# Layer norms beside two half-by-half projections: square sums and scaled tiles one product later, first sums one product later, inverse root in PSUM

## The reference

```python
mix = (gates[:, :, 0] * y_sb + gates[:, :, 1] * y_ret) @ w_mix_o[l]
x = layer_norm(DN_ALPHA * x + mix, ln1_g[l], ln1_b[l])
xa = memory_cross_attention(x, mem, w_mem_q[l], w_mem_kv[l], w_mem_o[l])
x = layer_norm(DN_ALPHA * x + xa, ln2_g[l], ln2_b[l])
f = x @ w_ffn_in[l]
ff = (jax.nn.silu(f[..., :FFN_HIDDEN]) * f[..., FFN_HIDDEN:]) @ w_ffn_out[l]
x = layer_norm(DN_ALPHA * x + ff, ln3_g[l], ln3_b[l])
```

## Time and profile before

| | us |
|---|---|
| median of 3 runs | 2077.23 (2077.11 to 2078.31) |
| profiled execution, its own time | 2074.83 |
| span of that execution | 2072.8 |
| mean granted clock of PE | 0.988 |
| PE busy | 1976.8 |
| DVE busy | 1100.5 |
| ACT busy | 729.9 |
| POOL busy | 949.3 |

### The profile page before, as it was taken

The page is one execution under the profiler, slowest core; times in us unless marked ns, Lnnn a source line. Parts: engine busy times, 40 slices in busy tenths (PEclk is TensorE's granted clock), DMA queues, the critical chain, the costliest instruction groups (busy, mean ns, idle before and its releaser), DMA issues. The chain is left out here.

```text
span 2072.8 us, 25775 instructions
## 1 busy us (share of the span) xinstructions
PE 1976.8 (95%) x10024; PEld 1638.4 (79%) x10024; DVE 1100.5 (53%) x1180; ACT 729.9 (35%) x1133; POOL 949.3 (46%) x519
## 2 busy tenths in 40 slices
PE   8999999999999999999989999989999999999986
PEld 6888888888777787888768887777888888888866
DVE  5667577400166565238873337877454455411646
ACT  2323224100055555312452224454433333422444
POOL 4243342433354454444575543565555555543423
PEclk9999999999999999999999999999999999999998
DMA  5022020122100000312322111242222222363452
GB/s 187 31 91 71 30 91 31 51 81 71 61 22 21 21 32 21 122 43 78 96 78 72 61 61 59 74 142 92 76 83 87 86 78 82 138 201 129 136 164 97
DMA packets 56538, 168.22 MB, mean 81 GB/s; under 512 B 5888, under 2 KB 12160, under 8 KB 55424
## 3 DMA queue, kind: packets, MB, share of 16 engines
q1 hardware_dynamic: 49648, 142.86, 20.7%
q10 hardware_dynamic: 6800, 24.12, 3.1%
HBM read 142.84 MB, written 24.12 MB: 81 GB/s over the span
## 5 line engine op out<-in xcount | busy, mean ns | idle before, releaser
L508 POOL TENSOR_TENSOR w_hi<-w_raw,one 128x1024 fp32r<-128x1024 f32 x68 | 133.6, 1965 | 467.1 <-PE unit L650 467.1
L650 PE MATMUL unit<-x_hi,w_hi 128*128 128x512 f32 x768 | 248.0, 394 | 13.2 <-DVE diag L1795 9.9
L660 PE MATMUL unit<-x_lo,w_hi 128*128 128x512 f32 x768 | 245.4, 390 | 0.4 <-POOL x_lo L527 0.4
L668 PE MATMUL unit<-x_hi,w_lo 128*128 128x512 f32 x768 | 190.4, 390 | 0.0
L650 PEld LDWEIGHTS unit<-x_hi,w_hi 128*128 128x128 f32 x768 | 144.3, 189 | 45.8 <-issue 11.6
L511 POOL TENSOR_TENSOR w_lo<-w_raw,w_hi 128x1024 fp32r<-128x1024 f32 x68 | 176.6, 2597 | 5.3
L660 PEld LDWEIGHTS unit<-x_lo,w_hi 128*128 128x128 f32 x768 | 144.1, 188 | 31.0 <-POOL x_lo L527 0.9
L668 PEld LDWEIGHTS unit<-x_hi,w_lo 128*128 128x128 f32 x768 | 144.6, 188 | 30.2
L572 POOL TENSOR_TENSOR w_lo<-w_raw,w_hi 128x1024 fp32r<-128x1024 f32 x46 | 112.8, 2451 | 101.3 <-ACT w_hi L1414 101.1
L590 POOL TENSOR_TENSOR beta<-beta,stick 128x128 f32<-128x128 f32 (+7 forms) x64 | 77.1, 1205 | 150.6 <-DVE stick L1936 150.6
L1936 DVE TENSOR_TENSOR_SCAN stick<-stick 128x128 f32<-128x128 f32 (+7 forms) x64 | 106.2, 1661 | 49.8 <-ACT stick L1344 49.8
(11 more groups left out here) (602 smaller groups left out, 5115.8 us busy)
## 6 DMA issues: line engine op xcount, KB each, us to landing
w_raw<-stream SPq DMA_DIRECT2D x157, 512.0 KB, 3.7
w_next<-stream SPq DMA_DIRECT2D x34, 512.0 KB, 4.4
hidden_store<-hidden SPq DMA_DIRECT2D x22, 512.0 KB, 2.6
h_raw<-hidden_store SPq DMA_DIRECT2D x44, 256.0 KB, 3.9
rope_sb<-rope ACTq DMA_DIRECT2D x8, 1024.0 KB, 4.9
w_next<-stream SPq DMA_DIRECT2D x12, 384.0 KB, 3.4
acc<-xT ACTq DMA_DIRECT2D x8, 512.0 KB, 10.3
ret_branch<-acc ACTq DMA_DIRECT2D x8, 512.0 KB, 2.6
```

The source lines that it names most:

```text
L508: pool.tensor_tensor(w_hi[s][:, 0:width], w_raw[:, s, 0:width], one[:].to_broadcast([P, width]), ALU.mult).then_inc(w_hi_done, 1)
L650: x = pe.matmul(out, w_hi[s][:, wk], hi[:, k, cols], start=k == 0, stop=False, skip_group_check=True)
L660: last = pe.matmul(out, w_hi[s][:, wk], lo[:, k, cols], start=False, stop=k == kts - 1 and x_lag > w_lag, skip_group_check=True)
L668: last = pe.matmul(out, w_lo[s][:, wk], hi[:, k, cols], start=False, stop=k == kts - 1 and x_lag <= w_lag, skip_group_check=True)
```

## The change

Five edits, the same in both norms except the last.

1. The square of block q is added to `total_sq` after the residual of block q+1, so a new function `add_square` is split from `residual`; the low parts of the totals go from after q = 7 to after q = 8, the last square of half 1 to the end.
2. `sums(m, 0)` goes from after product 8 to after product 9, and with it the high parts of the totals, mean square and root on ACT, variance and reciprocal on DVE, each one q later.
3. `TILES_BESIDE` spreads the 8 tiles over q = 10 to 15 with 1, 2, 1, 2, 1, 1 tiles, in place of 1, 2, 2, 2, 1 over 9 to 13. ACT takes a tile's steps two q after its entry in place of one, so that tiles 6 and 7 come after the loop, tile 6 ahead of and tile 7 among the weight pieces that follow; POOL's low parts of tiles 6 and 7 likewise.
4. The reciprocal root is written to `aux` bank 2 + half, in PSUM (where the mean square lay), and the scaling reads it there.
5. In `n1` the memory's high part on ACT goes from q = 15 to q = 12, its low part on DVE from q = 14 to q = 13.

```diff
--- before.py
+++ after.py
@@ -74,7 +74,7 @@
 SUMS = (S1, S2, S3, S4)
 RING = 4
 ADDS = KT - 1
-TILES_BESIDE = {9: (0,), 10: (1, 2), 11: (3, 4), 12: (5, 6), 13: (7,)}
+TILES_BESIDE = {10: (0,), 11: (1, 2), 12: (3,), 13: (4, 5), 14: (6,), 15: (7,)}
 TURN_ORDER = (2, 3, 0, 1)
 
 
@@ -194,7 +194,7 @@
             sb(st, "gap4", [P, 2, HALF])
             total_hi, total_lo, total_sq_hi, total_sq_lo = (
                 sb(st, n, [P, HALF], F32R) for n in ("total_hi", "total_lo", "total_sq_hi", "total_sq_lo"))
-            ln_mean2, ln_rstd = sb(st, "ln_mean2", [P, HALF]), sb(st, "ln_rstd", [P, HALF])
+            ln_mean2, ln_var = sb(st, "ln_mean2", [P, HALF]), sb(st, "ln_var", [P, HALF])
         with ExitStack() as st:
             t_hi, t_lo = {}, {}
             for j in (2, 3):
@@ -593,13 +593,23 @@
                         (single_lo if hd else single_hi)(FILL_SPLITS[g])
             split(CH_GSB + 1, CH_MIX + 2 - CH_GSB - 1, 8 * P)
             beside_residual(CH_MIX, CH_MEM, normed_lo)
-            for c in range(CH_MEM + 1, CH_MEM + 6):
+            normed_lo(KT - 2)
+            single_lo(CH_MEM + 1)
+            single_lo(CH_MEM + 2)
+            normed_lo(KT - 1)
+            for c in range(CH_MEM + 3, CH_MEM + 6):
                 single_lo(c)
             for q in range(KT, 2 * KT):
                 normed_lo(q)
             split(CH_MEM + 6, CH_MO + 2 - CH_MEM - 6, 8 * P)
             beside_residual(CH_MO, CH_FFN - 1, normed_part_lo)
-            for f in range(2 * RING):
+            form_lo(0)
+            form_lo(1)
+            normed_part_lo(KT - 2)
+            form_lo(2)
+            form_lo(3)
+            normed_part_lo(KT - 1)
+            for f in range(RING, 2 * RING):
                 form_lo(f)
             for q in range(KT, 2 * KT):
                 normed_part_lo(q)
@@ -939,7 +949,7 @@
                 for q in range(2, 2 * KT):
                     pe.wait_ge(unit_drained[q % 2], first // 2 + max(0, q // 2 - 1))
                     tiles(q, range(KT)).then_inc(unit_ready, 1)
-                    if q == KT:
+                    if q == KT + 1:
                         sums(m, 0)
 
             residual(n1, CH_MIX, U_MIX)
@@ -1436,7 +1446,7 @@
 
             def root(m, hf):
                 act.wait_ge(m.var, hf + 1)
-                act.activation(ln_mean2[:], ln_rstd[:], ACT.Sqrt).then_inc(m.std, 1)
+                act.activation(ln_mean2[:], ln_var[:], ACT.Sqrt).then_inc(m.std, 1)
 
             def beside_residual(m, which, chunk, last_chunk, tile, others):
                 for q in range(1, 2 * KT):
@@ -1448,12 +1458,12 @@
                     if q == KT - 1:
                         act.activation(root_table[:, which:which + 1], one[:], ACT.Sqrt)
                     square_of(m, q - 1)
-                    if q == KT:
+                    if q == KT + 1:
                         total_hi_parts(m, 0)
-                    if q == KT + 1:
+                    if q == KT + 2:
                         mean_square(m, 0)
                         root(m, 0)
-                    for k in TILES_BESIDE.get(q - 1, ()):
+                    for k in TILES_BESIDE.get(q - 2, ()):
                         tile(k)
                     if q in others:
                         others[q]()
@@ -1478,7 +1488,7 @@
                 for k in range(0, KT, 4):
                     act.activation(mem_hi[:, k:k + 4, :], mem_raw[:, k:k + 4, :], ACT.Copy).then_inc(mem_hi_done, 4)
 
-            beside_residual(n1, 0, CH_MIX, CH_MEM, normed_tile, {KT: load_memory, 2 * KT - 1: split_memory})
+            beside_residual(n1, 0, CH_MIX, CH_MEM, normed_tile, {KT: load_memory, KT + 4: split_memory})
 
             def mem_unit(s):
                 return unit[:, s, :].rearrange("p (a t) -> p a t", a=2)[:, :, 0:MEM]
@@ -1543,10 +1553,12 @@
                 if more:
                     queries_and_v(h, base + 4)
 
+            normed_tile(KT - 2)
             single_hi(CH_MEM + 1)
             square_of(n1, 2 * KT - 1)
             total_hi_parts(n1, 1)
             single_hi(CH_MEM + 2)
+            normed_tile(KT - 1)
             keys(0, U_MEM + 1)
             mean_square(n1, 1)
             single_hi(CH_MEM + 3)
@@ -1595,10 +1607,12 @@
                 form_hi_part(1)
 
             beside_residual(n2, 1, CH_MO, CH_FFN - 1, normed_part, {2 * KT - 1: first_forms})
+            normed_part(KT - 2)
             form_hi_part(2)
             form_hi_part(3)
             square_of(n2, 2 * KT - 1)
             total_hi_parts(n2, 1)
+            normed_part(KT - 1)
             for f in range(RING, 2 * RING):
                 form_hi_part(f)
             mean_square(n2, 1)
@@ -2020,6 +2034,9 @@
                     dve.wait_ge(m.total_added, ADDS * hf + n - 1)
                 dve.tensor_tensor(total, acc[:, 0, half(hf)] if n == 1 else total, r, ALU.add
                                   ).then_inc(m.total_added, 1)
+
+            def add_square(m, q):
+                hf, n = divmod(q, KT)
                 dve.wait_ge(m.squared, q + 1)
                 if n > 1:
                     dve.wait_ge(m.square_added, ADDS * hf + n - 1)
@@ -2035,12 +2052,12 @@
 
             def variance(m, hf):
                 dve.wait_ge(m.mean_sq, hf + 1)
-                dve.scalar_tensor_tensor(out=ln_rstd[:], in0=aux[:, 2 + hf, :], scalar=EPS, in1=ln_mean2[:],
+                dve.scalar_tensor_tensor(out=ln_var[:], in0=aux[:, 2 + hf, :], scalar=EPS, in1=ln_mean2[:],
                                          op0=ALU.add, op1=ALU.subtract).then_inc(m.var, 1)
 
             def invert(m, hf):
                 dve.wait_ge(m.std, hf + 1)
-                dve.reciprocal(ln_rstd[:], ln_mean2[:]).then_inc(m.inverted, 1)
+                dve.reciprocal(aux[:, 2 + hf, :], ln_mean2[:]).then_inc(m.inverted, 1)
 
             def center(m, q, freed):
                 hf, k = divmod(q, KT)
@@ -2052,7 +2069,7 @@
             def scale(m, q):
                 dve.wait_ge(m.inverted, q // KT + 1)
                 dve.wait_ge(m.centered, q + 1)
-                dve.tensor_tensor(ln_t[:, q % 4, :], ln_t[:, q % 4, :], ln_rstd[:], ALU.mult).then_inc(m.scaled, 1)
+                dve.tensor_tensor(ln_t[:, q % 4, :], ln_t[:, q % 4, :], aux[:, 2 + q // KT, :], ALU.mult).then_inc(m.scaled, 1)
 
             def residual_halves(m, first, freed):
                 for q in range(2 * KT):
@@ -2060,20 +2077,23 @@
                     if q < KT // 2:
                         split_a(m, 1, 2 * q)
                         split_a(m, 1, 2 * q + 1)
-                    if q == KT - 1:
+                    if q % KT > 1 or q == KT:
+                        add_square(m, q - 1)
+                    if q == KT:
                         total_lo_parts(m, 0)
-                    if q == KT:
+                    if q == KT + 1:
                         variance(m, 0)
                         invert(m, 0)
                     for k in TILES_BESIDE.get(q, ()):
                         center(m, k, freed)
                     for k in TILES_BESIDE.get(q, ()):
                         scale(m, k)
-                    if q == 2 * KT - 2 and m is n1:
+                    if q == 2 * KT - 3 and m is n1:
                         for k in range(0, KT, 4):
                             dve.wait_ge(mem_hi_done, k + 4)
                             dve.tensor_tensor(mem_lo[:, k:k + 4, :], mem_raw[:, k:k + 4, :], f32(mem_hi[:, k:k + 4, :]),
                                               ALU.subtract).then_inc(mem_split, 4)
+                add_square(m, 2 * KT - 1)
                 total_lo_parts(m, 1)
 
             def second_norm(m, freed):
```

## The result

The changed kernel takes **2061.82 us**, median of 4 runs (2060.21 to 2063.74); the kernel before took 2077.17 on the same chip (4 runs, 2076.45 to 2078.31). The ratio is 0.9926, 95% interval 0.9909 to 0.9943. The forecast was 2061.7, range 2053 to 2070.

What follows compares the result with a forecast made beforehand. PE, busy 95% of the span, was taken as the bound, so only its waits and half clock could yield time. Gains of 9.5 us (first norm) and 6.0 (second), 15.5 off the median 2077.23, gave 2061.7; range 2053 to 2070.

Steps and rivals of the forecast that it cites:

- Products: In both norms, products end earlier without waits for totals and weight chunks: 8.5 us in the first, 8.7 in the second.
- The chain by hand: First norm, DVE's steps from product 9: memory's low part starts at 1032.5, chunk 81's high part ends at 1045.1.
- What was added in the first norm: Moved work costs PE 1.6 us at the memory, 4.4 at chunk 81 and 2.3 of half clock: 8.3 us.
- Second norm: PE waits 4.1 us at the first FFN weights, 2.6 at the form blocks; pair 1 takes 6.4; gain 6.0.
- Root in PSUM: Both norms: every scaling falls from 1.19 to 0.68 us; the reciprocal into PSUM takes 3.35.
- Everything is covered: Rival, chance 0.20: DVE's additions miss POOL's splits, so it is in time for product 14; about 2053 us.
- The lag grows: Rival, chance 0.12: DVE falls another 3 to 4 us behind by product 14; about 2069 us.
- Slower: Rival, chance 0.03: scaling from PSUM is much longer than centering; up to 2094 us.
- the change does little: Rival, chance 0.04: POOL and ACT are already at their limit and waits only change names; 2074 to 2081 us.
- Sums one product later: 4.85 us per norm: Sums behind product 9 remove PE's 2.06 us wait for the totals, shorter waits and half clock: 4.85 us per norm.
- What ends these waits is DVE, then ACT: Step on both norms: DVE's scalings and block additions from SBUF run long beside POOL's weight splits of 2.44 us.
- Weight chunks waiting behind tiles: 3.1 and 3.3 us: With fewer tiles per product, PE's waits for weight chunks go: 3.1 us in the first norm, 3.3 in the second.

Runs made afterwards that it cites:

- Run 9: Changed kernel with the sums back behind product 8 and each square added with its own product, behind DVE's two splits: 2055.89 us, ratio 0.9893.
- run 3: Changed kernel with the tiles back at the old lots (1, 2, 2, 2, 1 from product 9 on): 2058.19 us, ratio 0.9896.
- run 4: Changed kernel with the memory's split back behind DVE's product 14 and ACT's q = 15: 2060.13 us, ratio 0.9906.
- run 10: The kernel of run 3 with SP's second FFN pair also issued ahead of the stores of tiles 6 and 7: 2058.41 us, ratio 0.9908.
- run 7: Changed kernel with SP's second pair of FFN weights issued ahead of the stores of tiles 6 and 7: 2054.91 us, ratio 0.9889.
- run 5: Changed kernel with tile 6 of the first norm behind chunk 81's split, on ACT and POOL: 2060.99 us, ratio 0.9916.
- run 6: Changed kernel with the memory's low part on POOL at q = 10 and 11 instead of DVE, high part at 9 and 10: 2055.9 us, ratio 0.9906.

## Why the prediction was right

Against the marks, nearly every step came out as it was worked.

- *Products.* Forecast 8.5 and 8.7 us sooner; 95.94 - 87.40 = 8.54 and 96.12 - 87.40 = 8.72. The sums wait for nothing.
- *The chain by hand.* The memory's low part was to start 85.4 us after the norm's first matmul (1032.5 - 947.13) and started at 1036.17, 85.22. Chunk 81's high part was to end at 1045.1, that is 98.0; it ended 97.9 after. DVE's and ACT's rows:

```profile
1036.17 5.62 DVE L2094 TENSOR_TENSOR mem_lo<-mem_raw,mem_hi 128x1024 fp32r<-128x1024 f32 x2
```

```profile
1043.15 0.63 ACT L1431 ACTIVATE square<-acc 128x512 f32<-128x512 f32 x1 [6.92 <-DVE acc L2028]
...
1047.80 1.04 ACT L1424 ACTIVATE w_hi<-w_raw 128x1024 fp32r<-128x1024 f32 x1
```

- *What was added in the first norm.* 1.6 + 4.4 + 2.3 forecast; 2.16 + 3.33 and 1.5 of half clock measured, 7.0 instead of 8.3. So the stretch gained 10.7, not 9.5. Mis-sized were the wait at chunk 81, 3.3 and not 4.4, and the half clock, 1.5 and not 2.3.
- *Second norm.* Pair 1's bounds were 5.9 to 7.5 and 6.4 taken. The high parts of both pairs on ACT:

```profile
1346.93 1.15 ACT L1595 ACTIVATE w_hi<-w_raw 128x512 fp32r<-128x512 f32 x2 [0.82 <-DMA w_raw<-stream]
...
1359.35 2.20 ACT L1595 ACTIVATE early_hi<-w_next 128x512 fp32r<-128x512 f32 x4 [5.62 <-DMA w_next<-stream]
```

  The pairs issued at 1340.93 and 1353.46 were used 6.0 and 5.9 us later. The wait at the FFN weights was 4.3 (4.1 forecast), at the form block 2.8 (2.6), the gain 7.0 (6.0). By the Trainium skill's fit for a load (SBUF — State Buffer, The DMA setup-cost knee) the estimate is 4.4 us, 1.5 to 1.6 under both; the measurement decides.
- *Root in PSUM.* The reciprocal took 3.36 us, as costed, and the scaling as long as the centering, 681 ns in the middle; its shortest from SBUF alone was 677. By the estimate from the Trainium skill (Perfetto Trace Analysis, Optimizing Scalar/DVE Operations) it would have grown by 65 ns; the trace shows 4.
- *Rivals.* "Everything is covered" needed product 11's addition to miss POOL's split; it met it (2.70 us at 1020.65). "The lag grows" needed waits for weights before product 15; there are none over 0.2 us. "Slower" needed a long scaling; "the change does little" a gain under 3 us.
- *Outside.* 3.4 us lost in the memory heads and 1.4 gained behind the form blocks were not forecast; with 2.2 too little in the norms they nearly cancel. That the total came out within 0.2 us of the forecast is luck, then; the two norms were forecast to 1.2 and 1.0 us.

**What the prediction got wrong is what each edit is worth**, which its total does not need. "Sums one product later: 4.85 us per norm" is the price of the wait; the cure was credited to the delay. Run 9 shows that the sums can stand at product 8 with no wait once DVE's splits miss POOL, and that the kernel with the earlier sums and root is 3.5 and 2.3 us faster; how much of that the root's place gives, and how much the pieces that miss POOL behind it, it doesn't separate. The step behind it reads "What ends these waits is DVE, then ACT", and it named blocked scalings and block additions, but not the splits at L1998, which with three of the additions made DVE late for the totals. "Weight chunks waiting behind tiles: 3.1 and 3.3 us" was credited to the thinner lots; run 3 shows that with the root in PSUM the old lots cost 3.0 and 1.8 us of products, and still bring PE to the form blocks 2.95 us sooner. In the two norms together the thinner lots lose 1.6 us, by the medians 3.6. For the memory's move the sum had it about right: 7.9 gained, 8.3 added, and run 4 shows next to nothing.

## What to carry to other kernels

Forecast the whole schedule on the engine that is late, in its order, and a chain by hand can be right to a few tenths of a microsecond over 98 us; what each of several edits is worth has to be measured one at a time. When PE waits for a chain, list every instruction of the late engine that lasts longer than its shortest twin, back to where it was last on time: reordering two of its own instructions so that they miss the other engine may do what moving the consumer does. And look at what a DMA queue has in front of a load that matters: moving one load ahead of two stores gave 3.4 us. With the old lots, where those stores came early anyway, it gave 0.4. Last, compare stretch by stretch: effects of 1 to 3 us drown in totals that differ by up to 7 us between executions of one kernel (run 10).

## What the runs showed of the hardware

The same waits do not always cost the same. In each of the first three memory heads PE waits 2.2 to 2.5 us for prob, in every kernel here. PE by stretches (stretch, its length, PE busy and instructions, granted clock, DMA share, GB/s) around the first three of these waits, in the changed kernel, then in run 10:

```profile
1100.00:1110.00 10.00, 9.29 (x55) 0.83 0.30 98
...
1150.00:1160.00 10.00, 9.12 (x53) 0.83 0.30 104
...
1200.00:1210.00 10.00, 8.76 (x52) 0.83 0.31 104
```

```profile
1098.00:1108.00 10.00, 9.24 (x61) 1.00 0.33 106
...
1147.00:1157.00 10.00, 9.42 (x61) 1.00 0.32 105
...
1196.00:1206.00 10.00, 9.60 (x55) 0.83 0.32 105
```

After waits of equal length PE falls to its 1.2 GHz level behind all three in one execution and behind one in the other; the heads take 153.9 us and 150.6. Single runs of one kernel differ by it too: run 7's were 2060.09 us at a mean clock of 0.987 and 2053.5 to 2055.0 at 0.991 to 0.992. What decides it stays open. The same holds at chunk 81: behind a wait of 2.3 us in run 9, and of 2.1 in run 5 (1.6 waited at chunk 80 before it), the granted clock is 0.50; behind 2.2 in run 6 it stays at 1.00.

Not expected either was how much of DVE's time this costs where nobody looks: beside products 1 to 3 of the first norm three pairs of splits took 3.50 us instead of 1.28 before, and one pair 5.31 after, all with both inputs in SBUF, while none of the 64 scalings and centerings with one input in PSUM left 677 to 689 ns.
